# A mixture-of-experts encoder layer: the order in which the 64 experts take their turns, sorted by size instead of mixed

## The chip, the cores and the metric

The kernel runs on one core of one Trainium2 chip. The metric is the device time of one execution in microseconds (us), the median of several runs. The core's engines are TensorE (PE in the profile), VectorE (DVE), ScalarE (ACT), GpSimd (POOL) and SyncE (SP). Everything is float32.

## What is computed

The reference is one bidirectional encoder layer on 512 + 256 tokens of width 1024. Its first part (gated MLP, a gated linear recurrence over 8 heads, projections, layer norm) is not touched by the change. The part that matters here is the routed mixture of experts:

```python
scores = jax.nn.sigmoid((xt @ w_router).astype(f32))      # 768 tokens x 64 experts
...                                                       # 4 of 8 groups, then the top 6 experts of each token
hb = jax.nn.silu(xb @ w_e_gate[e]) * (xb @ w_e_up[e])     # w_e_gate, w_e_up: 1024 x 256 per expert
return (hb @ w_e_down[e]).astype(f32) * g[:, None]        # w_e_down: 256 x 1024 per expert
...
y = moe_ffn(...)                                          # sum over the 6 experts of a token, plus one shared expert
return layer_norm(ALPHA * x + y, ln2_g, ln2_b)
```

768 tokens times 6 choices are 4608 rows, which are spread unevenly over the 64 experts.

## The kernel before, in words

The kernel ranks the experts on the chip by how many rows each one got (rank 0 is the fullest). The program is fixed beforehand, with room by rank: `rooms()` (L53) gives rank 0 one unit of 32 rows, ranks 1 to 10 four units, ranks 11 to 42 three, and ranks 43 to 63 two. That is 179 units. The units are laid end to end in the order in which the experts take their turns (`TURN`, L67, which `ranks_in_turn()` returns), and cut into 45 **rounds** of 128 rows (`NR`, L69). What does not fit into a room (here the rest of rank 0) is done in blocks of 128 rows after the rounds.

Words used below: a *turn* is the place of an expert in that order, 0 to 63, whatever its rank. *Small*, *middle* and *large* experts are those with two, three and four units.

A round on TensorE (L1068 to L1076) is: `up(t)`, the gate and up products of the round's experts (L1036); `down(t - 1)`, the down products of the round before (L1062); `hidden_turn(t)`, two transposes (L1047); `gathered_turn(t + 2)`, eight transposes of gathered rows (L1023). The array is used in column pieces: a round that belongs to one expert is done in one piece of 128 rows, one whose borders are even in two pieces of 64, any other in four pieces of 32 (`pieces`, L151). The pieces of one step stand in different columns of the array.

The weights of an expert are one load of its gate and up matrices (`load_gate_up`, L569) and one of its down matrix (`load_down`, L572). Both go into one of six places (`NB = 6`: rA, rCD, rB, ew, the upper half of rEF, the upper half of rCD, in that order); turn j has place j % 6. All of them are issued by SP on one queue, in this order:

```python
            for t in range(NR):
                for j in range(E - NB):
                    if last_round(j) == t:
                        sp.wait_ge(gu_filled, t + 1)
                        load_gate_up(expert_in_turn(j + NB), j % NB)
                for j in range(E - NB):
                    if last_round(j) == t - 1:
                        sp.wait_ge(y_filled, t)
                        load_down(expert_in_turn(j + NB), j % NB)
```

So the gate-up load of turn j + 6 is issued when `up` of the last round of turn j is done, and its down load one round later. `up(t)` waits for the gate-up loads of all experts of its round (L1033), `down(t)` for their down loads (L1058). The first six turns are loaded before the rounds begin.

GpSimd gathers the 128 rows of a round from HBM (L1813) and scatters its 128 result rows (L1819), on a queue of its own; places in a room that no token fills move no bytes. After the rounds comes the block of the rest, then the six results of each token are loaded back and summed, and the last layer norm is done.

In the order before, `first` is four small experts, `mixed` spreads the other 17 small, the 32 middle and the 10 large ones evenly over the run, and rank 0 comes last.

Of the kernel before, what the change touches and what calls it, by code (L numbers as in the profile page):

```python
# [57 lines left out]
def ranks_in_turn():  # L58

    large, middle, small = list(range(10, 0, -1)), list(range(11, 43)), list(range(63, 42, -1))  # L60
    first, small = small[:4], small[4:]
    mixed = sorted(((i + 0.5) / len(g), r) for g in (large, small, middle) for i, r in enumerate(g))
    return first + [r for _, r in mixed] + [0]


ROOMS = rooms()
TURN = ranks_in_turn()  # L67
STARTS = [sum(ROOMS[r] for r in TURN[:j]) for j in range(E + 1)]
NR = -(-STARTS[E] // UNITS)  # L69
# [1812 lines left out]
```

How the kernel before makes its waits and increments, by code:

```python
    def link(self, ins):  # L170
        self.n += 1
        ins.then_inc(self.sem, 1)
        self.eng.wait_ge(self.sem, self.n)
# [1 line left out]
    def restart(self):  # L175
        self.eng.wait_ge(self.sem, self.n)
        self.eng.sem_clear(self.sem)
        self.n = 0
# [300 lines left out]
        @block.sync  # L480
# [8 lines left out]
            def load_x(i):
                src = d["x_prompt"][i * P:(i + 1) * P, :] if i < NTP else \
                    d["x_sample"][(i - NTP) * P:(i - NTP + 1) * P, :]
                sp.dma_start(x_in[:, i, :], src).then_inc(s_x[i], 16)
            load_x(1)
            for n, c0 in enumerate((C_U, C_V, C_I, C_I + 512, C_G)):
                if n >= 2:
                    sp.wait_ge(g_filled, NT * (n - 1))
                sp.dma_start(strip[n % 2], w_in[:, :, c0:c0 + 512]).then_inc(s_strip[n % 2], 16)
                if n == 0:
                    for i in range(2, NT):
                        load_x(i)
                    sp.dma_start(ws_sb, d["a_ws"].rearrange("g t s -> t g s")).then_inc(s_misc, 16)
                    sp.dma_start(sbt[:, :], d["a_sb"]).then_inc(s_misc, 16)
                    sp.dma_start(nrow, d["hg_norm_g"].to_broadcast([P, D])).then_inc(s_misc, 16)
                    sp.dma_start(lbraw[0:4 * H, :], d["hg_lb_logits"].rearrange(
                        "a l (h k) -> (a l h) k", h=H)).then_inc(s_misc, 16)
            sp.wait_ge(x1_ready, NT)
            for i in range(NT):
                sp.dma_start(d["x1_dram"][i * P:(i + 1) * P, :], x_in[:, i, :]).then_inc(x1_stored, 16)
```

## Time and profile before

| | |
|---|---|
| median of 3 runs | 1817.21 us (1816.81 to 1818.77) |
| the profiled execution, its own time | 1814.63 us |
| its span, first to last instruction | 1812.5 us |
| TensorE busy | 95% of the span |
| mean granted TensorE clock | 0.989 |
| bytes moved by DMA | 330.78 MB |
| of them on SP's queue / on GpSimd's queue | 292.05 MB / 37.77 MB |

The span is the one to reckon in; the profiled execution's own time is 2.1 us above it. The times inside the trace are microseconds from the start of the span. The rounds lie between 1174 and 1728 us, the block of the rest and the sum behind them.

### The profile page before, as it was taken

How to read it: one execution, taken by the hardware profiler on the slowest of the kernel's cores; microseconds unless marked ns; L12 is line 12 of the kernel's file. 1: busy time of each engine (PE TensorE's matmuls, PEld its weight loads, DVE VectorE, ACT ScalarE, POOL GpSimd, SP SyncE). 2: the span in 40 equal slices, each digit the busy share in tenths (PEclk: the TensorE clock that was granted, in tenths of full speed). 3: DMA queues.
4: the chain of work that ended last, by engine and by line, in shares of the span. 5: the costliest groups of instructions: out<-in, count | busy, mean ns of one | idle time of the engine just before them, and what ended most of it. 6: DMA issues, size and time to landing. Idle time of an engine off the chain costs nothing.

```text
span 1812.5 us, 20130 instructions
## 1 busy us (share of the span) xinstructions
PE 1729.1 (95%) x7961; PEld 888.6 (49%) x7961; DVE 651.7 (36%) x965; ACT 297.0 (16%) x436; POOL 150.9 (8%) x147
## 2 busy tenths in 40 slices
PE   6999999999999999999999999999999999898966
PEld 3444456666666656556555544533333333333322
DVE  5011019888888874300111687400000000000018
ACT  1111112111111111112000121022222222121210
POOL 0000000000000000000000111511111111111122
PEclk9999999999999999999999999999999999999988
DMA  6114101101101001111116204799999999999857
GB/s 225 46 47 162 47 24 35 35 24 35 35 23 35 23 0 35 46 58 41 41 52 238 88 24 171 289 375 423 422 423 424 422 423 421 418 412 402 320 226 310
DMA packets 104980, 330.78 MB, mean 182 GB/s; under 512 B 8496, under 2 KB 64848, under 8 KB 86736
## 3 DMA queue, kind: packets, MB, share of 16 engines
q1 hardware_dynamic: 91520, 292.05, 40.8%
q0 software_dynamic: 13392, 37.77, 5.3%
q8 instruction: 49, 0.80, 0.2%
q14 instruction: 19, 0.16, 0.0%
HBM read 307.24 MB, written 33.55 MB: 188 GB/s over the span
## 4 chain that ended last, share of the span: by engine, by line
PE 79%; DVE 9%; DMA 9%; issue 1%; ACT 1%; SPq 0%; POOL 0%; DVEq 0%; POOLq 0%; ACTq 0%
PE pA L1036 14%; PE pg L669 11%; PE pg L696 10%; PE pg L819 9%; PE pB L1062 6%; PE pB L850 5%; DMA ew<-w_e_gate_up 4%; PE pB L899 2%; PE pA L899 2%; PE pA L842 2%; PE pg L709 2%; PE pB L752 2%; DMA rEF<-w_e_gate_up 2%; DMA rA<-w_e_gate_up 2%; PE pg L1023 2%; PE pA L789 1%
## 5 line engine op out<-in xcount | busy, mean ns | idle before, releaser
L696 PE MATMUL pg<-rA,hw 128*128 128x384 f32 x768 | 259.6, 486 | 0.7 <-ACT aTr L1172 0.7
L1036 PE MATMUL pA<-rCD,aTr 128*32 128x512 f32 (+2 forms) x720 | 209.2, 600 | 12.1 <-DMA rA<-w_e_gate_up 10.0
L1755 DVE TENSOR_TENSOR rows<-rows,pA 128x256 f32<-128x256 f32 x45 | 18.9, 421 | 529.8 <-ACT rows L1280 529.8
L669 PE MATMUL pg<-rEF,rA 128*128 128x512 f32 x448 | 195.0, 597 | 3.1 <-ACT rCD L1151 3.1
L696 PEld LDWEIGHTS pg<-rA,hw 128*128 128x128 f32 x768 | 140.5, 190 | 84.1 <-ACT aTr L1172 0.9
L819 PE MATMUL pg<-rA,hw 128*128 128x384 f32 x512 | 165.3, 486 | 0.0
L669 PEld LDWEIGHTS pg<-rEF,rA 128*128 128x128 f32 x448 | 85.6, 192 | 109.8 <-issue 109.8
L819 PEld LDWEIGHTS pg<-rA,hw 128*128 128x128 f32 x512 | 97.2, 190 | 67.6
L1036 PE MATMUL pA<-rA,aTr 128*32 128x512 f32 (+2 forms) x384 | 124.3, 606 | 0.0
L1036 PE MATMUL pA<-rB,aTr 128*32 128x512 f32 (+1 forms) x368 | 107.7, 599 | 4.2 <-DMA rEF<-w_e_gate_up 4.0
L1036 PE MATMUL pA<-ew,aTr 128*32 128x512 f32 (+1 forms) x352 | 107.7, 605 | 0.0
L1798 POOL TENSOR_SCALAR rEF<-rB 128x1024 f32<-128x1024 f32 x6 | 16.6, 2771 | 1073.2 <-DVE rB L1352 1073.2
L1062 PE MATMUL pB<-rCD,rows 128*32 128x512 f32 (+2 forms) x360 | 105.1, 595 | 0.0
L1036 PE MATMUL pA<-rEF,aTr 128*32 128x512 f32 (+1 forms) x352 | 100.6, 599 | 0.0
L1036 PEld LDWEIGHTS pA<-rCD,aTr 128*32 128x32 f32 (+2 forms) x720 | 58.4, 120 | 76.8 <-issue 73.6
L850 PE MATMUL pB<-rB,hw 128*128 128x384 f32 x256 | 83.9, 486 | 0.0
L1165 ACT ACTIVATE rEF<-pg 128x384 f32<-128x384 f32 x48 | 23.5, 490 | 283.5 <-PE pg L696 283.5
L850 PEld LDWEIGHTS pB<-rB,hw 128*128 128x128 f32 x256 | 48.6, 190 | 33.9
L1280 ACT ACTIVATE rows<-pA 128x256 f32<-128x256 f32 x45 | 17.2, 383 | 290.4 <-PE pA L1036 290.4
L1062 PE MATMUL pB<-rA,rows 128*32 128x512 f32 (+2 forms) x192 | 61.6, 595 | 0.0
L1539 DVE TENSOR_TENSOR ew<-pA,rEF 128x768 f32<-128x768 f32 x8 | 7.7, 957 | 141.3 <-PE pA L842 141.3
L1473 DVE TENSOR_TENSOR rEF<-rEF 128x768 f32<-128x768 f32 x56 | 53.7, 959 | 7.7 <-PE pA L752 1.6
(318 smaller groups left out, 2344.0 us busy)
## 6 DMA issues: line engine op xcount, KB each, us to landing
rCD<-w_e_gate_up SPq DMA_DIRECT2D x21, 2048.0 KB
rA<-w_e_gate_up SPq DMA_DIRECT2D x11, 2048.0 KB
rB<-w_e_gate_up SPq DMA_DIRECT2D x11, 2048.0 KB
ew<-w_e_gate_up SPq DMA_DIRECT2D x11, 2048.0 KB, 32.7
rEF<-w_e_gate_up SPq DMA_DIRECT2D x11, 2048.0 KB
rCD<-w_e_down SPq DMA_DIRECT2D x21, 1024.0 KB
hw<-w_in SPq DMA_DIRECT2D x40, 512.0 KB, 4.1
rA<-w_e_down SPq DMA_DIRECT2D x11, 1024.0 KB
```

The costliest lines, as they stand in the source:

```text
L669: last = mm(big_bank(fill), x1T[:, c, i * P:(i + 1) * P], strip[n % 2][:, c, :], start=(c == 0), stop=(c == KC - 1))
L696: last = mm(pg[:, n * 512:n * 512 + HALF], hw3[m][:, c, :], x1T[:, c, n * HALF:(n + 1) * HALF], start=(c == 0), stop=(c == KC - 1))
L709: last = mm(pg[:, (i % 2) * 512:(i % 2) * 512 + 512], x1T[:, c, i * P:(i + 1) * P], g_strip[c // 4][:, c % 4, :], start=(c == 0), stop=(c ...
L752: last = mm(buf[:, o:o + P], kt[:, i * P:(i + 1) * P], qt[:, i * P:(i + 1) * P], start=True, stop=True)
L819: last = mm(pg[:, n * 512:n * 512 + HALF], hw3[m][:, c, :], x1T[:, c, n * HALF:(n + 1) * HALF], start=(c == 0), stop=(c == KC - 1))
L842: last = mm(pA[:, n * 512:n * 512 + HALF], hw3[0][:, c, :], aT[:, c, n * HALF:(n + 1) * HALF], start=(c == 0), stop=(c == 3))
L850: last = mm(pB[:, n * 512:n * 512 + HALF], hw3[1][:, c, :], rT[:, c, n * HALF:(n + 1) * HALF], start=(c == 0), stop=(c == KC - 1))
L899: last = mm(pair[i % 2][:, n * 512:(n + 1) * 512], mT[:, c, i * P:(i + 1) * P], wo_sb[:, c, n * 512:(n + 1) * 512], start=(c == 0), stop=( ...
L1023: last = tr(pg[:, c * P:(c + 1) * P], xg[t % 2][:, c:D:KC], ident)
L1036: last = mm(gu[n][o:o + w, :], xT[n][:, c, o:o + w], at(gate_up_home(j % NB)[0], gate_up_home(j % NB)[1] + c * F, [[2 * D, 2], [1, F]]), s ...
L1062: last = mm(pB[o:o + w, m * 512:(m + 1) * 512], hT[n][:, k, o:o + w], wd[j % NB][:, k, m * 512:(m + 1) * 512], start=(k == 0), stop=(k == 1))
L1473: link(v.tensor_tensor(both("P", half, half, 0), both("P", half, half, 0), total(half, half - 1, half), ALU.mult))
```

## The change

`ranks_in_turn()` returns the ranks from 63 down to 0: the 21 small experts, then the 32 middle ones, then the 10 large ones, then rank 0, which is last in both.

```diff
@@ -60,7 +60,7 @@
     large, middle, small = list(range(10, 0, -1)), list(range(11, 43)), list(range(63, 42, -1))
     first, small = small[:4], small[4:]
     mixed = sorted(((i + 0.5) / len(g), r) for g in (large, small, middle) for i, r in enumerate(g))
-    return first + [r for _, r in mixed] + [0]
+    return list(range(63, -1, -1))
```

Rooms, number of rounds, places and the block of the rest stay as they are. What moves is which turns fall into a round, and so when SP issues which load. Rounds 0 to 9 now hold two whole small experts each; from there to round 33 three rounds hold four middle experts; from round 34 on each round holds the halves of two large ones.

On SP, the loads that are issued after rounds 2 to 5. Before, from the gate-up load of turn 10 on (rEF and so on are the places; the rows left out are the waits and the loads of the expert's number into a register):

```order
L569 DMA rEF<-w_e_gate_up 128x4096
...
L572 DMA rB<-w_e_down 128x2048
...
L572 DMA ew<-w_e_down 128x2048
...
L569 DMA rCD<-w_e_gate_up 128x4096
...
L569 DMA rA<-w_e_gate_up 128x4096
...
L572 DMA rEF<-w_e_down 128x2048
...
L569 DMA rCD<-w_e_gate_up 128x4096
...
L572 DMA rCD<-w_e_down 128x2048
```

The same stretch now:

```order
L569 DMA rEF<-w_e_gate_up 128x4096
...
L569 DMA rCD<-w_e_gate_up 128x4096
...
L572 DMA rB<-w_e_down 128x2048
...
L572 DMA ew<-w_e_down 128x2048
...
L569 DMA rA<-w_e_gate_up 128x4096
...
L569 DMA rCD<-w_e_gate_up 128x4096
...
L572 DMA rEF<-w_e_down 128x2048
...
L572 DMA rCD<-w_e_down 128x2048
```

Two gate-up loads and two down loads now follow each round, where before it was one or two of each.

On TensorE, round 4: before, it is one large expert in one piece, between the down products of a round in four pieces:

```order
L1023 MATMUL pg<-con,hw 128x128 x7
L1036 MATMUL pA<-rCD,aTr 128x512 [waits w_gate_up_loaded1,hidden_ready,gathered_T_ready]
L1036 MATMUL pA<-rCD,aTr 128x512 x7
L1062 MATMUL pB<-rCD,rows 32x512 [waits w_down_loaded0,w_down_loaded5,y_ready,hiddenT_ready]
L1062 MATMUL pB<-rA,rows 32x512 x3
```

The same round now, two small experts in two pieces:

```order
L1023 MATMUL pg<-con,hw 128x128 x7
L1036 MATMUL pA<-rB,aTr 64x512 [waits w_gate_up_loaded2,w_gate_up_loaded3,hidden_ready,gathered_T_ready]
L1036 MATMUL pA<-ew,aTr 64x512
L1036 MATMUL pA<-rB,aTr 64x512
L1036 MATMUL pA<-ew,aTr 64x512
```

`up(4)` waited for one load, that of turn 7; it now waits for two, those of turns 8 and 9. Over all rounds the pieces go from 136 to 123.

## Rows read from the trace of the kernel before

**Rows 1.** The span in 40 slices of 45.3 us (from the page).

```profile
PE   6999999999999999999999999999999999898966
...
PEclk9999999999999999999999999999999999999988
DMA  6114101101101001111116204799999999999857
GB/s 225 46 47 162 47 24 35 35 24 35 35 23 35 23 0 35 46 58 41 41 52 238 88 24 171 289 375 423 422 423 424 422 423 421 418 412 402 320 226 310
```

**Rows 2.** Windows: length, busy time by engine, clock, DMA share, GB/s.

```profile
1130.00:1135.00 5.00, 4.88 (x13) 2.37 (x14) 2.42 (x8) 0.38 (x1) 0.00 (x0) 1.00 1.04 437
...
1120.00:1160.00 40.00, 37.23 (x129) 22.11 (x128) 27.04 (x64) 2.47 (x7) 23.51 (x34) 1.00 1.01 424
1185.00:1405.00 220.00, 220.00 (x1646) 80.65 (x1642) 8.00 (x19) 48.69 (x73) 36.74 (x37) 1.00 1.01 423
...
1576.00:1690.00 114.00, 107.85 (x730) 40.31 (x728) 3.79 (x9) 23.70 (x36) 16.21 (x16) 0.98 0.99 406
```

**Rows 3.** Timeline of TensorE: start, duration; L1047 once a round; last, round 44.

```profile
1182.24 0.41 PE L1047 MATMUL pX<-con,rows 128*128 128x128 f32 x2 [1.03 <-DVE rows L1755]
...
1217.47 0.44 PE L1047 MATMUL pX<-con,rows 128*128 128x128 f32 x2
...
1229.17 0.44 PE L1047 MATMUL pX<-con,rows 128*128 128x128 f32 x2
...
1405.46 0.44 PE L1047 MATMUL pX<-con,rows 128*128 128x128 f32 x2
1423.53 0.44 PE L1047 MATMUL pX<-con,rows 128*128 128x128 f32 x2
...
1712.82 0.62 PE L1036 MATMUL pA<-rB,aTr 128*32 128x512 f32 x2
```

**Rows 4.** Timeline of TensorE: the four `up`s with a wait for weights, rounds 20, 33, 38, 40.

```profile
1410.08 1.09 PE L1036 MATMUL pA<-rCD,aTr 128*64 128x512 f32 x1 [3.28 <-DMA rA<-w_e_gate_up]
...
1573.49 1.09 PE L1036 MATMUL pA<-rCD,aTr 128*64 128x512 f32 x1 [6.71 <-DMA rA<-w_e_gate_up]
...
1636.23 0.59 PE L1036 MATMUL pA<-rCD,aTr 128*32 128x512 f32 x1 [1.86 <-DMA rCD<-w_e_gate_up]
1663.88 0.59 PE L1036 MATMUL pA<-rB,aTr 128*32 128x512 f32 x1 [4.03 <-DMA rEF<-w_e_gate_up]
```

**Rows 5.** Timeline of SP's queue: gate-up loads of turns 6 and 63, then the rest's.

```profile
1181.96 0.34 SPq L569 DMA_DIRECT2D rA<-w_e_gate_up  x1
...
1674.53 0.34 SPq L569 DMA_DIRECT2D ew<-w_e_gate_up  x1
...
1700.22 0.34 SPq L569 DMA_DIRECT2D rEF<-w_e_gate_up  x1
```

**Rows 6.** DMA view: GpSimd's queue (packets, MB, share), then size of a load.

```profile
q0 software_dynamic: 13392, 37.77, 5.3%
...
rCD<-w_e_gate_up SPq DMA_DIRECT2D x21, 2048.0 KB
...
rCD<-w_e_down SPq DMA_DIRECT2D x21, 1024.0 KB
```

**Rows 7.** Windows around the waits of rounds 20 and 38, columns as in rows 2.

```profile
1405.00:1410.00 5.00, 1.79 (x14) 1.14 (x10) 0.00 (x0) 2.30 (x3) 2.02 (x2) 0.91 1.01 424
1410.00:1415.00 5.00, 4.92 (x12) 1.65 (x14) 0.00 (x0) 0.00 (x0) 0.00 (x0) 0.50 1.00 418
1415.00:1420.00 5.00, 5.00 (x26) 1.55 (x25) 0.00 (x0) 0.00 (x0) 0.00 (x0) 0.91 1.04 435
1635.00:1640.00 5.00, 3.77 (x36) 1.44 (x40) 0.00 (x0) 0.46 (x1) 2.03 (x2) 1.00 1.00 421
```

**Rows 8.** Timeline of TensorE: `up(4)` in one piece, the start of `up(5)` in four.

```profile
1218.64 7.03 PE L1036 MATMUL pA<-rCD,aTr 128*128 128x512 f32 x16
1225.60 0.62 PE L1062 MATMUL pB<-rCD,rows 128*32 128x512 f32 x1
...
1230.43 0.63 PE L1036 MATMUL pA<-rB,aTr 128*32 128x512 f32 x3
1230.45 0.62 PE L1036 MATMUL pA<-ew,aTr 128*32 128x512 f32 x1
...
1237.43 3.70 PE L1062 MATMUL pB<-rCD,rows 128*128 128x512 f32 x8
```

## The prediction

> **What bounds the kernel now.** I read the 40 slices first. TensorE shows a 9 almost everywhere, which suggests a kernel bound by TensorE. But from slice 27 on DMA is at 9 as well and moves 421 to 424 GB/s [rows 1]. So in the rounds there are two candidates, and the windows say how full the second is: from 1185 to 1405 us the share is 1.01 at 423 GB/s, and it was 424 GB/s in the stretch before, when only whole transfers and no gathers were under way [rows 2]. That is a full queue. The timeline then says who waits. From round 0 to round 19 TensorE goes at its own pace: (1405.46 - 1182.24) / 19 = 11.75 us a round [rows 3]. After that four `up`s wait for a gate-up load, 3.28 + 6.71 + 1.86 + 4.03 = 15.9 us [rows 4]. All four rounds begin or hold the turn whose load came last. So TensorE lives on a lead (six experts loaded beforehand) until round 20, and from there on the weights are the limit.
>
> The loads can be reckoned as one account. A gate-up load is 2.10 MB, a down load 1.05 MB [rows 6]. The queue begins to fill with turn 6 at 1181.96 us [rows 5] and is full from 1185. The wait that ends at 1573.49 (round 33, turn 48) needs the gate-up loads of turns 6 to 48 and, issued ahead of it, the down loads of turns 6 to 46: 43 x 2.097 + 41 x 1.049 = 133.2 MB. Beside them GpSimd's queue moves 37.77 MB in all [rows 6], which is 4608 rows of 4 KB there and back; routing the reference's own inputs and filling the rooms in the old order, the gathers of rounds 2 to 35 and the scatters of rounds 0 to 31 are 6717 rows, 27.5 MB. Together 160.7 MB in 1573.5 - 1185 = 388.5 us, **413.6 GB/s** effective. The same account for the wait that ends at 1410.08 (turn 30: 25 and 23 loads, 16.9 MB of rows) gives 415 GB/s, and for 1663.88 (turn 58: 53 and 51 loads, 33.2 MB) 413 GB/s. One rate explains three waits [rows 4], so this is the account to use.
>
> **What the change costs TensorE itself.** It goes from 136 to 123 pieces. `up(4)` in one piece takes from 1218.64 to 1225.60; `up(5)` in four pieces from 1230.43 to 1237.43 [rows 8]: 7.0 us either way, since the pieces of a step run side by side. Round 0, in two pieces, is followed by rounds of the same 11.7 us; from 1217.47 to 1229.17 [rows 3] is 11.70. So fewer pieces gain nothing, and I put them at 0. The bounds are the spread of a round, 0.05 us x 45 = 2 us to either side. Number of rounds, bytes, gathers and scatters are the same.
>
> **What it costs the queue.** Nothing is added, but the demand moves. Per round, with 0.82 MB of gathered and scattered rows (37.77 / 46), and at 413.6 GB/s:
> - small section, rounds 0 to 9, two experts: 6.29 + 0.82 = 7.11 MB, 17.2 us against TensorE's 11.75;
> - middle section, to round 33, 4 experts in 3 rounds: 4.19 + 0.82 = 5.01 MB, 12.1 us;
> - large section, round 34 on, one expert: 3.15 + 0.82 = 3.97 MB, 9.6 us.
>
> So the queue is the limit in the first two sections, and TensorE in the last. There the queue has capacity left over, but every load that it could do ahead of time is held back by the six places. Capacity that lies idle at the end can't be brought forward; that is the loss.
>
> Now the last point at which the queue decides, round 33 (turns 51 and 52). SP issues ahead of it the gate-up loads of turns 6 to 52 and the down loads of turns 6 to 49: 47 x 2.097 + 44 x 1.049 = 144.7 MB; rows gathered and scattered, filled in the new order, 6571, 26.9 MB; in all 171.6 MB. At 413.6 GB/s that is 414.9 us, so `up(33)` starts at 1185 + 414.9 = 1599.9 us. Eleven rounds at 11.75 us follow, TensorE-bound: `up(44)` starts at 1729.2. Before, it started at 1712.82 [rows 3]. **The rounds end 16.4 us later.**
>
> Checked from the other side. `up(10)` needs 16 gate-up and 12 down loads, 46.1 MB, and 8.2 MB of rows: 131.3 us, 1316.3. At TensorE's pace it would start at 1218.6 + 6 x 11.75 = 1289.1. So about 27 us are lost in rounds 5 to 10, some 5 us in each, after the lead is used up; the middle section loses 1599.9 - 1316.3 - 23 x 11.75 = 13 us, mostly where the first middle experts come and then 1 to 2 us in every third round. That is 40 us against the 24 that rounds 20 to 40 lose now (15.9 waiting, the rest at a lower clock).
>
> **The clock.** A wait costs more than its length: round 20 takes 1423.53 - 1405.46 = 18.07 us, 3.28 of waiting and 3.0 beyond the usual 11.75 [rows 3, 4]. The granted clock shows why: 0.50 (the 1.2 GHz level) just after the wait, back to 1.00 some ten us on; the wait of 1.86 us left it at 1.00 [rows 7]. In the small section a round with such a loss is 14.8 us of work in 17.2 us of loading: hidden, while the queue stays full. It stays full, because at the start of `up(t)` four more loads of its two next rounds are already queued. In the middle the waits are 1 to 2 us, like the one that cost nothing. So the clock adds 0; what its cover is worth if gone is a rival below.
>
> **Behind the rounds.** The rest's load now goes out after round 41's transposes, at about 1704 instead of 1700 [rows 5], and is first needed some 40 us later, behind `up(44)` and the last down products: 0. The tail from `up(44)` to the end is the same work, 99.7 us.
>
> **The sum.** 16.4 us (queue) + 0 (pieces) + 0 (clock) + 0 (tail). Against the profiled execution, 1814.6 + 16.4 = 1831.0; the median of the runs shown lies 2.6 higher, so 1817.2 + 16.4 = **1833.6 us**. The rate is what is unsure. At 423 GB/s, the full queue's reading [rows 2], `up(33)` starts at 1590.7 and the change costs 7 us, 1824; at 406, the reading of 1576 to 1690 [rows 2], 1607.7 and 24 us, 1841. I take 413.6, since only it reproduces the waits.
>
> **Rivals.**
> - *The clock drops again and again in the middle section too.* There the queue leaves TensorE only 0.35 us a round, 8 us in all. If each of the eight rounds that begin two experts waited long enough to lose 3.0 us, that is 24 - 8 = 16 us more: 1850. For it: such waits come right behind rounds at the low clock. Against it: they are expected at 1 to 2 us, and 1.86 us left the clock up [rows 7]. It decides once the waits reach the 3.28 us of rows 4. The Trainium skill ("TensorE: Matmul & The Clock Gate", the section on HAM oscillation) describes this pattern, a kernel that waits for DMA at every tile and starts every burst of matmuls throttled; by that rule the time would be the 1850 just worked out. The trace agrees at 3.28 us and not at 1.86. 10%.
> - *The queue is faster in the small section, and it comes out faster than before.* Weights then make up nearly nine tenths of the bytes, in long rows, and gathers are few. The best 5 us of the trace show 437 GB/s [rows 2]. At that rate `up(33)` starts at 1577.7, the rounds end 5.9 us earlier than now, 1811. The turning point is 430.5 GB/s. Against it: over 40 us of weights alone it was 424, the same as with gathers [rows 2]. 6%, half of it near no change.
> - *The waits are not the bytes' but SP's, which issues late.* Then 24 us of waiting and low clock could vanish with a more even pattern, 1793. Against it: the DMA share is 1.01 through the waits [rows 7]. 2%.
>
> **How the numbers follow.** The forecast has 82%. A measurement of this kernel can tell about 0.2% (3.6 us) from no change. Faster by more: 3% + 2% = 5%. Within: 3%. Slower: 82% + 10% = 92%. The range is that of the forecast's rate, 1824 to 1841, and 1 to 2 us more for the bound of the pieces: 1823 to 1843. It leaves out the three rivals, 18%.
>
> **What would show it.** Right: between 1240 and 1320 us TensorE is busy some two thirds of the time and waits about 5 us in each round for a gate-up load, with a granted clock below 1.00; the next larger wait is in round 11 or 12; the transposes L1047 then come every 12.1 us on average up to round 33, with waits of 1 to 2 us in every third; `up(33)` starts near 1600; after it no wait, 11.75 us a round, and a DMA share that falls below 0.9. Wrong: an `up(10)` before 1300 (rate), a round over 12.5 us after round 34 (TensorE), waits over 3 us in the middle (clock), or a tail that differs from 99.7 us.

## The result and the profile after

| | before | after | after, timed again (run e0) |
|---|---|---|---|
| median | 1817.99 us (4 runs, 1816.81 to 1818.88) | 1828.79 us (4 runs, 1825.63 to 1830.23) | 1826.14 us (5 runs) beside 1816.64 (9 runs) |
| ratio to before, 95% interval | | 1.006 (1.0046 to 1.0074) | 1.0052 (1.0039 to 1.0066) |
| span of the profiled execution | 1812.5 us | 1826.6 us | 1823.8 us |

The sorted order is slower by 10.8 us, and by 9.5 us when timed again. The forecast was 16.4 us.

The page of the changed kernel, to be laid beside [rows 1]; a slice is now 45.7 us:

```profile
PE   6999999999999999999999999998789999999967
...
PEclk9999999999999999999999999999999999999988
DMA  6114101110110001111117005599999999999557
GB/s 224 46 46 161 46 23 35 35 35 23 34 34 23 23 1 34 57 46 41 52 52 276 35 35 235 216 421 425 423 422 423 423 424 422 423 419 401 210 203 332
```

The slices are counted from 0. In TensorE's row the slices of the rounds that show less than a 9 have moved from 34 and 36 to 27, 28 and 29, right behind the start of the rounds, and the queue's slices 37 and 38 are down to 210 and 203 GB/s, from 320 and 226. That is the picture of a queue that is full early and idle late.

The timeline of TensorE in the changed kernel, every wait over 0.6 us in the rounds (start, duration, in brackets the idle time and who ended it), and L1047 of rounds 0, 6, 7, 33 and 44:

```profile
1185.28 0.41 PE L1047 MATMUL pX<-con,rows 128*128 128x128 f32 x2 [1.03 <-DVE rows L1755]
...
1246.86 0.61 PE L1036 MATMUL pA<-rA,aTr 128*64 128x512 f32 x1 [1.74 <-DMA rCD<-w_e_gate_up]
...
1257.31 0.44 PE L1047 MATMUL pX<-con,rows 128*128 128x128 f32 x2
...
1265.23 1.09 PE L1036 MATMUL pA<-rB,aTr 128*64 128x512 f32 x1 [6.60 <-DMA ew<-w_e_gate_up]
...
1278.32 0.44 PE L1047 MATMUL pX<-con,rows 128*128 128x128 f32 x2
...
1282.18 0.61 PE L1036 MATMUL pA<-rEF,aTr 128*64 128x512 f32 x1 [2.54 <-DMA rCD<-w_e_gate_up]
1298.86 1.08 PE L1036 MATMUL pA<-rA,aTr 128*64 128x512 f32 x1 [4.89 <-DMA rCD<-w_e_gate_up]
...
1315.91 0.61 PE L1036 MATMUL pA<-rB,aTr 128*64 128x512 f32 x1 [2.37 <-DMA ew<-w_e_gate_up]
1339.60 1.09 PE L1062 MATMUL pB<-rB,rows 128*64 128x512 f32 x1 [4.67 <-DMA ew<-w_e_down]
...
1525.56 0.63 PE L1036 MATMUL pA<-rCD,aTr 128*32 128x512 f32 x3 [1.10 <-ACT aTr L1273]
...
1562.76 0.63 PE L1036 MATMUL pA<-rCD,aTr 128*32 128x512 f32 x3 [1.74 <-DMA rA<-w_e_gate_up]
...
1599.58 0.63 PE L1036 MATMUL pA<-ew,aTr 128*32 128x512 f32 x3 [1.37 <-DMA rEF<-w_e_gate_up]
...
1610.02 0.44 PE L1047 MATMUL pX<-con,rows 128*128 128x128 f32 x2
...
1739.61 0.44 PE L1047 MATMUL pX<-con,rows 128*128 128x128 f32 x2
```

The long waits stand where the prediction put them: `up` of rounds 6 to 10, then round 11 (`down(10)` behind `up(11)`). Behind them the prediction had 1 to 2 us in every third round; there is none over 0.6 us up to round 26, then one of 1.1 to 1.7 us in rounds 27, 30 and 33, and none for a load behind that. The one of round 27 is put down to ScalarE here and to a gate-up load in run e0 (1.72 us). From L1047 of round 33 to that of round 44 it is 129.6 us, TensorE's pace. The clock, in windows of the changed kernel (columns as in [rows 2]):

```profile
1260.00:1265.00 5.00, 0.00 (x0) 0.00 (x0) 0.00 (x0) 0.00 (x0) 1.35 (x2) 0.88 0.99 415
1265.00:1270.00 5.00, 4.77 (x12) 1.64 (x14) 0.00 (x0) 0.00 (x0) 0.00 (x0) 0.50 1.02 428
...
1187.00:1315.90 128.90, 110.76 (x522) 43.57 (x519) 3.79 (x9) 24.82 (x37) 18.57 (x19) 0.95 1.01 423
1187.00:1599.60 412.60, 385.40 (x2563) 143.73 (x2560) 13.47 (x32) 86.62 (x129) 64.49 (x64) 0.98 1.01 423
...
1590.00:1740.00 150.00, 148.31 (x826) 55.74 (x818) 5.47 (x13) 32.90 (x50) 22.27 (x22) 1.00 0.82 337
```

Up to round 33 the queue is full at 423 GB/s, whether TensorE works or waits, at the high clock or at the low one. From 1590 us on its share is 0.82: this is the capacity that can't be used.

Taken apart, with the same marks in both traces:

| part | before | after | difference | forecast |
|---|---|---|---|---|
| L1047 of round 0 to that of round 44 | 541.0 | 554.3 | +13.3 | +16.4 |
| from there to the end of the span | 89.25 | 87.0 | -2.2 | 0 |
| sum | | | +11.1 | +16.4 |

The profiled execution began its rounds 3.0 us late (1185.28 against 1182.24 in [rows 3]), which the change has nothing to do with: in run e0, the same kernel, it is 1182.60, and the two parts are 554.2 and 87.0 us again.

### The profile page after: what moved, and what is told of

Its sections match the earlier page's. It is cut to its first block, busy times and chain, and to the rows that moved or that the text cites. A ratio compares the mean times of both kernels' runs of the same rounds, so it can differ in the third digit from the quotient of the medians.

```text
span 1826.6 us, 19496 instructions
## 1 busy us (share of the span) xinstructions
PE 1734.1 (95%) x7649; PEld 893.8 (49%) x7649; DVE 647.3 (35%) x965; ACT 297.2 (16%) x436; POOL 151.0 (8%) x147
## 4 chain that ended last, share of the span: by engine, by line
PE 78%; DMA 10%; DVE 9%; issue 1%; ACT 1%; SPq 0%; POOL 0%; DVEq 0%; POOLq 0%; ACTq 0%
PE pA L1036 13%; PE pg L669 11%; PE pg L696 10%; PE pg L819 9%; PE pB L1062 7%; PE pB L850 5%; DMA rA<-w_e_down 2%; DMA ew<-w_e_down 2%; PE pB L899 2%; PE pA L899 2%; PE pA L842 2%; DMA rA<-w_e_gate_up 2%; DMA rCD<-w_e_gate_up 2%; PE pg L709 2%; PE pB L752 2%; PE pg L1023 2%
## 5 line engine op out<-in xcount | busy, mean ns | idle before, releaser
L1036 PE MATMUL pA<-rCD,aTr 128*64 128x512 f32 (+1 forms) x640 | 215.1, 599 | 2.8 <-DMA rA<-w_e_gate_up 1.7
L1036 PE MATMUL pA<-rA,aTr 128*64 128x512 f32 (+1 forms) x320 | 116.0, 604 | 6.6 <-DMA rCD<-w_e_gate_up 6.6
L1036 PE MATMUL pA<-rB,aTr 128*32 128x512 f32 (+1 forms) x352 | 108.7, 602 | 9.0 <-DMA ew<-w_e_gate_up 9.0
L1036 PE MATMUL pA<-ew,aTr 128*32 128x512 f32 (+1 forms) x336 | 108.7, 603 | 1.5 <-DMA rEF<-w_e_gate_up 1.4
L1062 PE MATMUL pB<-rCD,rows 128*64 128x512 f32 (+1 forms) x320 | 108.4, 594 | 0.3 <-DMA rA<-w_e_down 0.3
L1036 PE MATMUL pA<-rEF,aTr 128*32 128x512 f32 (+1 forms) x320 | 99.0, 594 | 2.5 <-DMA rCD<-w_e_gate_up 2.5
L1036 PEld LDWEIGHTS pA<-rCD,aTr 128*64 128x64 f32 (+1 forms) x640 | 61.4, 124 | 61.7 <-issue 58.4
L1062 PE MATMUL pB<-rB,rows 128*32 128x512 f32 (+1 forms) x176 | 57.3, 613 | 5.8 <-DMA ew<-w_e_down 4.7
L1062 PE MATMUL pB<-rA,rows 128*64 128x512 f32 (+1 forms) x160 | 57.8, 594 | 0.0
## 6 DMA issues: line engine op xcount, KB each, us to landing
ew<-w_e_gate_up SPq DMA_DIRECT2D x11, 2048.0 KB, 34.5
```

What stands on the lines that cost most here:

```text
L1036: last = mm(gu[n][o:o + w, :], xT[n][:, c, o:o + w], at(gate_up_home(j % NB)[0], gate_up_home(j % NB)[1] + c * F, [[2 * D, 2], [1, F]]), s ...
L1062: last = mm(pB[o:o + w, m * 512:(m + 1) * 512], hT[n][:, k, o:o + w], wd[j % NB][:, k, m * 512:(m + 1) * 512], start=(k == 0), stop=(k == 1))
```

## The experiments

**Which end of the order costs?** The changed kernel is timed once more, and beside it three orders that keep or move one kind of experts each. They replace the last line of `ranks_in_turn()`.

Run e0, the changed kernel again:

> The changed kernel once more, timed in more rounds. The account of bytes, with the rate that the changed kernel's own waits show (0.417 instead of 0.4136 MB per us), gives 10 to 14 us over the kernel before. If the first timing (+10.8 us) was low by chance, the prediction's 16 us should come out.

Measured: +9.5 us, ratio 1.0052 (1.0039 to 1.0066). Half a microsecond below what the account allows, and well below the forecast's 16. The first timing was not low by chance.

Run e1, only the large ones last:

```diff
-    return list(range(63, -1, -1))
+    mixed = sorted(((i + 0.5) / len(g), r) for g in (small, middle) for i, r in enumerate(g))
+    return first + [r for _, r in mixed] + large + [0]
```

> Only the large experts are put last; the small ones stay mixed with the middle ones. Theory (account of bytes): the queue must have delivered the same weights by round 33 as in the sorted order, so the rounds end as late as there or 2 to 3 us later: +12 to +19 us over the kernel before, with waits of 3 to 4 us in every fourth round from round 12 to 33. Rival (the run of small experts with its long waits and the low clock is what costs): without that run the loss goes, 0 to +4 us.

Measured: 1837.3 us, +20.7, ratio 1.0115 (1.01 to 1.013). The rival is out: without a run of small experts the loss doesn't go, it doubles. It is also 2 us above my range. The timeline of TensorE has these waits among others (L1037 is the L1036 of the other kernels):

```profile
1316.59 1.09 PE L1037 MATMUL pA<-rCD,aTr 128*64 128x512 f32 x1 [4.49 <-DMA rB<-w_e_gate_up]
...
1370.78 1.09 PE L1037 MATMUL pA<-rCD,aTr 128*64 128x512 f32 x1 [4.12 <-DMA rB<-w_e_gate_up]
...
1426.00 1.08 PE L1037 MATMUL pA<-rCD,aTr 128*64 128x512 f32 x1 [3.57 <-DMA rB<-w_e_gate_up]
...
1569.11 1.03 PE L1063 MATMUL pB<-rB,rows 128*32 128x512 f32 x1 [4.32 <-DMA rEF<-w_e_down]
...
1623.30 1.03 PE L1063 MATMUL pB<-rB,rows 128*32 128x512 f32 x1 [2.31 <-DMA rEF<-w_e_down]
```

The last wait is not `up(33)` for a gate-up load but `down(33)` for a down load (L1063 here), which SP issues behind two more gate-up loads. By the account `down(33)` needs 179.2 MB in this order, against 176.9 in the sorted one. So where two experts begin in the round after, the down loads must be in the account too.

That does not explain the time, though. At the 0.417 MB per us of run e0's account, 179.2 MB have landed after 430 us, at 1614, and the rounds would end some 14 us later than before (an estimate from this account), inside my range. `down(33)` started at 1623.30, and the rounds ended 23.0 us later in the traces. Up to there the queue was full:

```profile
1184.40:1623.30 438.90, 405.16 (x2886) 147.74 (x2881) 14.32 (x34) 88.94 (x133) 67.18 (x67) 0.98 1.01 421
```

That is 184.8 MB, 5.6 more than the account asks for at this point. Why the queue had moved so much beyond what was awaited is open, and with it the last microseconds of this run.

Run e2, only the small ones first:

```diff
-    return list(range(63, -1, -1))
+    mixed = sorted(((i + 0.5) / len(g), r) for g in (large, middle) for i, r in enumerate(g))
+    return first + small + [r for _, r in mixed] + [0]
```

> Only the small experts are put first; middle and large ones are mixed behind them. Theory (account): the same waits in rounds 6 to 10 as in the sorted order, about 27 us, and then demand of 42 experts in 34 rounds is 11.2 us a round, below TensorE's 11.75, so no wait behind round 11: +7 to +12 us, less than the sorted order. Rival (all of the loss comes from the idle queue under the large experts at the end): about 0.

Measured: 1825.51 us, +8.9, ratio 1.0044 (1.003 to 1.0057). Inside the theory's range. Its waits of rounds 6 to 10 are 1.29, 6.80, 3.69, 3.99 and 3.85 us, close to those of the sorted order in run e0 (1.81, 6.58, 3.79, 3.43 and 3.66), the last in the rounds ends at 1355.15, and from there to the last round it goes at TensorE's pace:

```profile
1315.58 1.08 PE L1037 MATMUL pA<-rB,aTr 128*64 128x512 f32 x1 [3.85 <-DMA ew<-w_e_gate_up]
1339.68 1.08 PE L1063 MATMUL pB<-rB,rows 128*64 128x512 f32 x1 [3.90 <-DMA ew<-w_e_down]
1355.15 0.59 PE L1063 MATMUL pB<-ew,rows 128*32 128x512 f32 x1 [2.36 <-DMA rEF<-w_e_down]
1738.63 0.62 PE L1063 MATMUL pB<-rB,rows 128*32 128x512 f32 x2 [1.15 <-ACT rows L1288]
```

So either end alone costs 9 us or more, and the two together are not a sum: both are the same account read at different rounds.

Run e3, small ones last:

```diff
-    return list(range(63, -1, -1))
+    return first + middle + large + small + [0]
```

> Four small experts first as before, then the middle ones, the large ones, and the other 17 small ones last. Theory (account): the queue can run ahead only by its six places, is held back under the large experts, and waits come in the last three rounds only; the rounds end 5 to 8 us earlier than before: -4 to -8 us. Rival (two experts in a round cost their waits wherever they stand): the same 5 us in each of eight rounds as in the sorted order, +10 us or more.

Measured: 1808.6 us, -8.0, ratio 0.9952 (0.9939 to 0.9966): faster than both kernels. The same two experts a round wait at the end as well, but only in the last four rounds (three were expected), and no round before them waits:

```profile
1657.53 1.09 PE L1036 MATMUL pA<-rB,aTr 128*64 128x512 f32 x1 [3.09 <-DMA ew<-w_e_gate_up]
1675.29 1.09 PE L1036 MATMUL pA<-rEF,aTr 128*64 128x512 f32 x1 [4.43 <-DMA rCD<-w_e_gate_up]
1692.55 0.61 PE L1036 MATMUL pA<-rA,aTr 128*64 128x512 f32 x1 [2.57 <-DMA rCD<-w_e_gate_up]
1708.54 1.07 PE L1036 MATMUL pA<-rB,aTr 128*32 128x512 f32 x2 [4.20 <-DMA ew<-w_e_gate_up]
```

In the traces the rounds are 5.4 us shorter than before (535.6 us against 541.0 from L1047 of round 0 to that of round 44), and 2.2 us lie behind them, in the tail (below). In this order nine rounds of large experts also take 11.4 us instead of 11.8 (last section), some 3 us. How much of the 5.4 us they give, and how much the queue, was not separated.

**Is it the bytes?** In both orders, the loads of turns 6 to 63 are cut to a quarter. Every instruction stays.

```diff
-            def load_gate_up(e, n):
-                sp.dma_start(gate_up[n], d["w_e_gate_up"][bass.ds(e, 1), :, :].rearrange("e p n -> (e p) n")).then_inc(s_wgu[n], 16)
+            def load_gate_up(e, n, part=1):
+                sp.dma_start(gate_up[n][:, 0:4 * D // part], d["w_e_gate_up"][bass.ds(e, 1), :, 0:4 * D // part].rearrange("e p n -> (e p) n")).then_inc(s_wgu[n], 16)
...
-                        load_gate_up(expert_in_turn(j + NB), j % NB)
+                        load_gate_up(expert_in_turn(j + NB), j % NB, 4)
```

and the same in `load_down`.

> Sorted order; of the weights of turns 6 to 63 only the first quarter of each load is brought in, and the rest of the place keeps older weights (the products are of those). All instructions stay. Theory (bytes): the small section then needs 2.4 MB a round, far below what the queue moves in 11.75 us, so no wait for weights in any round, TensorE's pace from 0 to 44, and a time within 3 us of its sister in the old order. Rival (SP's issuing, or the number of loads and semaphores in a round, is the limit): the waits of rounds 6 to 10 stay.

> The kernel before with the same quarter loads for turns 6 to 63. Theory (bytes): its four waits (15.9 us) and the 8 us of low clock behind them go: -22 to -26 us against the kernel before. It has 136 pieces where the sorted one has 123: if pieces cost nothing, both quarter kernels end within 2 us of each other; if they cost, this one is slower.

Measured: 1790.38 us sorted (ratio to before 0.9851, 0.9834 to 0.9867) and 1793.71 us mixed (0.9873, 0.9856 to 0.9889). No `up` and no `down` waits for a load in either. So the waits are for bytes, not for SP's issuing or the number of loads. Without them L1047 of round 44 comes 517.4 us after that of round 0 in the sorted order and 518.3 in the mixed one: thirteen pieces less are worth 0.9 us when nothing else limits. The medians are 3.3 us apart, more than the 2 us I had expected; 2 us of it lie behind the rounds (below).

```profile
1184.40 0.41 PE L1047 MATMUL pX<-con,rows 128*128 128x128 f32 x2 [1.03 <-DVE rows L1755]
...
1701.79 0.44 PE L1047 MATMUL pX<-con,rows 128*128 128x128 f32 x2
```

(The timeline of the sorted one.)

**Where is TensorE the limit, and where not?** In the sorted order with whole loads again, 2.6 us of TensorE work are added to each of five rounds, once under the small experts and once under the large ones; the repeated products are overwritten by the real ones. The first kernel does it in rounds 5 to 9, as shown; the other has `range(36, 41)` in its place.

```diff
+                for c in range(3 if t in range(5, 10) else 0):
+                    for j, o, w in pieces(t):
+                        mm(gu[n][o:o + w, :], xT[n][:, c, o:o + w],
+                           at(gate_up_home(j % NB)[0], gate_up_home(j % NB)[1] + c * F, [[2 * D, 2], [1, F]]),
+                           start=True, stop=True)
                 for c in range(KC):
```

> Sorted order; in rounds 5 to 9 the first three chunks of the gate-up products are done once more ahead of the real ones, 6 steps of 0.43 us or 2.6 us of TensorE work a round, 13 us in all. Theory (the queue is the limit there): the waits shrink by as much and the time stays, 0 to +3 us over the sorted order. Rival (TensorE with its low clock sets the small section): +13 us or more.

> Sorted order; the same extra work in rounds 36 to 40, under the large experts. Theory (TensorE is the limit there, the queue idles): all of it shows, +13 us over the sorted order. Rival (the queue is still the limit at the end): 0 to +3 us.

Measured: 1827.81 us in rounds 5 to 9, 1.7 us over run e0, and 1843.18 us in rounds 36 to 40, 17.0 us over it. In the traces, from L1047 of round 0 to that of round 44 (L1052 in these kernels), it is 553.9 and 566.9 us against e0's 554.2: -0.3 and +12.8. What the medians show beyond that, about 2 and 4 us, lies behind the rounds (the tail, below) and in the scatter of single runs. The 13 us are swallowed whole under the small experts and show whole under the large ones. One window over the small section, of e0 and then of e6:

```profile
1236.00:1346.00 110.00, 87.98 (x444) 34.33 (x442) 2.95 (x7) 18.81 (x28) 14.12 (x14) 0.91 1.01 424
```

```profile
1236.00:1346.00 110.00, 96.42 (x496) 39.18 (x496) 2.95 (x7) 18.79 (x28) 13.38 (x14) 0.94 1.01 424
```

TensorE is busy 8.4 us longer and the queue moves the same 424 GB/s.

**An order that beats both.** In the account the queue must have enough to do until the last round without an early shortage. So the order stays mixed, and six of the small experts are held back for the end:

```diff
     first, small = small[:4], small[4:]
+    small, last = small[:-6], small[-6:]
     mixed = sorted(((i + 0.5) / len(g), r) for g in (large, small, middle) for i, r in enumerate(g))
-    return first + [r for _, r in mixed] + [0]
+    return first + [r for _, r in mixed] + last + [0]
```

> The mixed order with one difference: six of the small experts are held back for the end, the other eleven stay mixed with middle and large ones. Theory (account of bytes): the mixed part demands 51 experts in the first 41 rounds or so, less than before, so the waits of rounds 20 to 40 go, and the queue stays busy to the end with the lead spent only in the last three rounds; waits of 6 us at round 42 and 1 us at round 44 are left, and the rounds end 9 to 12 us earlier: -9 to -12 us against the kernel before, a little faster than all small ones last (-8 us). Rival (the end needs no small experts, what counts is that the large ones aren't last): as fast as the kernel before, 0 to -3 us.

Measured: 1804.26 us beside 1816.86, -12.6 us, ratio 0.9926 (0.9912 to 0.994). In the traces the rounds are 10.0 us shorter (531.0 against 541.0), inside the expected 9 to 12, and 1.7 us lie in the tail. Two waits for weights are left in the rounds, 8.20 us in round 42 and 1.76 in round 44:

```profile
1678.03 1.09 PE L1037 MATMUL pA<-rEF,aTr 128*64 128x512 f32 x1 [8.20 <-DMA rCD<-w_e_gate_up]
...
1705.69 0.62 PE L1037 MATMUL pA<-rB,aTr 128*32 128x512 f32 x2 [1.76 <-DMA ew<-w_e_gate_up]
```

## Why the prediction was right, and where its size was off

The forecast had the direction, the two limits and the place of the loss. The sum was 5.6 us too high: 3.1 us of that lie in the rounds and 2.2 in the tail.

**What bounds it.** Right. The quarter loads take all waits away, and the share of 1.01 up to round 33 stays when TensorE gets more to do.

**Pieces, 0.** Right in effect: 0.9 us with the queue out of the way, inside the 2 us allowed.

**`up(33)` and the eleven rounds behind it.** The step held. Counted from L1047 of round 0, `up(33)` was forecast at 1599.9 - 1182.2 = 417.7 us and came at 414.3 (414.2 in e0). The rounds behind took 129.6 us instead of 129.3. In absolute times the forecast, 1599.9 and 1729.2, looks exact (1599.58 and 1729.03), but this is luck: the execution began its rounds 3.0 us late.

**The rate, 413.6 GB/s for all sections.** This is the term that was mis-sized, by 3.4 us. `up(10)` was forecast 134.1 us after L1047 of round 0 and came after 130.6 (130.7 in e0); from there to `up(33)` 283.6 was forecast and 283.7 measured. So the whole miss lies in the small section. The windows show why. Up to the wait for turn 48 the kernel before moved 422 GB/s x 389.5 us = 164.4 MB (window 1184 to 1573.5), but my account held only the 160.7 MB that had to be there. 3.7 MB were transfers that were under way or done beyond those waited for, and I had booked them as a lower rate. In the changed kernel the same difference is 54.5 - 54.3 = 0.2 MB at `up(10)` (1187 to 1315.9) and 174.5 - 171.6 = 2.9 MB at `up(33)`. The queue's own reading, 423, was the right rate, with an allowance for what lies beyond; it was near nothing at `up(10)`, in the fifth round in a row with a wait, and 5.6 MB at the last wait of e1. Which transfers make it up, and what sets its size, is not shown. I had this rate as the optimistic end of the range; it is right for the first section only.

**The tail, 0.** Off by 2.2 us. From L1047 of round 44 to the end it is 87.0 us in the changed kernel, e0, e3 and e4, and 87.5 in e8, but 89.25 before, and 88.7 to 89.1 in e1, e2, e5, e6 and e7. Runs e6 and e7 have the sorted order and the longer tail, so the order alone does not set it. Where the tail is long, the loads of the result rows land later: the load into rEF 34.6 us after its issue before, 33.4 after, and GpSimd waits 6.36 instead of 5.05 us for the fourth. The cause is open, and no experiment was made on it.

**The clock, 0.** Right in the small section: the run with 13 us more work shows that there is more cover than the clock takes; 12.3 us of waits for loads are still left in its rounds 7 to 11. For the rival, with losses that aren't covered, e1 is the nearest case. There 53 experts fall on 34.5 rounds, (4.83 + 0.82) / 0.4136 = 13.7 us a round; the cover is only 1.9, and rounds 12, 16 and 20 take 17.7, 17.6 and 18.4 us with waits of 4.49, 4.12 and 3.57 us: 1.5, 1.7 and 3.1 us beyond wait and pace. The granted clock in the 5 us behind these waits was 0.73, 0.69 and 0.50. That these losses lengthened the run is not shown: the queue was full up to its last wait. Nor does the length of a wait alone tell what it costs: in e1 waits of 2.58 and 3.10 us cost 0.2 and left the clock at 1.00, while one of 2.86 us (round 27, right behind the one of 3.10) cost 1.9 at a clock of 0.66, and in e3 one of 3.09 us cost 1.6 at 0.68. The section on HAM oscillation of the Trainium skill ("TensorE: Matmul & The Clock Gate") says that a burst of matmuls after a long enough DMA wait begins throttled. The traces agree for the three long waits of e1 and for the 6.60 us of the changed kernel's round 7 (0.50 from 1265 to 1270).

**The other rivals.** That the queue could be faster in the small section was half right: 424.6 GB/s by the account (54.3 MB in the 127.9 us from 1188), not the 430.5 needed for a draw. That SP issues late is ruled out by the quarter loads.

**What would show it.** TensorE was busy 77% of 1240 to 1320 us (eight windows of 10 us), not two thirds; the waits were shorter than forecast by what the rate was, and busy time at the low clock counts as busy. Two of the other signs did not come as written. The transposes L1047 came every 12.0 us from round 12 to round 33, but with waits in three of those rounds and not in every third. And the tail from `up(44)` is 97.6 us, not 99.7, which I had named as a sign of being wrong. The rest came: a clock of 0.91 in those 80 us, the next long wait in round 11, no round over 12.3 us after round 34, and a DMA share of 0.82 at the end.

## What to carry to other kernels

Where a queue and an engine are both nearly full, an order of work is an account over time: sum up the bytes that must have landed at each step and look for the last step at which they are late; what the engine does behind it is the price. In this kernel, work that needs much weight for little computing belonged where a lead has been built up, at the end, and not at the beginning, and work with little weight was worst when it came last, since a queue with six places can't run ahead under it; best was a mixed order with only a few of the heavy loads held back for the end. Take the queue's rate from the windows in which it is full, and keep what it has moved beyond the awaited transfer as a separate item (0.2 to 5.6 MB here).

## What the runs showed of the hardware that was not expected

A round whose `up` and `down` are both in one piece of 128 rows is shorter: in e3, where ten rounds are aligned so, L1047 comes every 11.4 us, against 11.7 in two pieces.

```profile
1503.27 0.38 PE L1047 MATMUL pX<-con,rows 128*128 128x128 f32 x2
...
1504.38 7.03 PE L1036 MATMUL pA<-rB,aTr 128*128 128x512 f32 x16
1511.25 3.60 PE L1062 MATMUL pB<-rCD,rows 128*128 128x512 f32 x8
1514.68 0.38 PE L1047 MATMUL pX<-con,rows 128*128 128x128 f32 x2
```

The kernel before showed only single operations of that kind between others in four pieces [rows 8], where no difference could be seen. And the tail has lengths 2 us apart in kernels with the same work there, as told above; the cause is open.
